# Expert weights as whole 2 MB units instead of pairs of 1 MB halves, with ring slots handed out whole

## The chip, the core and the metric

The kernel runs on one core of one Trainium2 chip. The metric is the device time of one execution in microseconds, given as the median of several runs. All data is 32-bit floating point.

## The reference, cut to what matters

The reference is a first network block of two layers (a gated-linear-attention and state-space mixer, then a dense feed-forward in layer 0 and a mixture of experts in layer 1), followed by a second block (Hyena convolution, neighbourhood attention, and a product-key expert lookup called PEER). The change lies in the mixture of experts:

```python
D_MODEL = 1024; SEQ = 256; D_FF = 3584; N_EXPERTS = 8; TOP_K = 2

def swiglu(t, w_gate, w_up, w_down):
    return (jax.nn.silu(t @ w_gate) * (t @ w_up)) @ w_down

def moe_swiglu(h, router_w, w_gate, w_up, w_down):
    t = h.reshape(bsz * seq, d)
    logits = (t @ router_w).astype(jnp.float32)
    top_v, top_i = lax.top_k(logits, TOP_K)
    top_p = jax.nn.softmax(top_v, axis=-1)
    gates = jnp.sum(jax.nn.one_hot(top_i, N_EXPERTS) * top_p[..., None], axis=1)
    out = jnp.zeros_like(t)
    for e in range(N_EXPERTS):
        out = out + gates[:, e:e + 1] * swiglu(t, w_gate[e], w_up[e], w_down[e])
    return out.reshape(bsz, seq, d)
```

Each of the 8 experts has three weight matrices of 1024 x 3584 values, so the stage reads 352 MB of weights once.

## The kernel before, in words

**Steps and units.** The hidden width 3584 of each expert is cut into 7 pieces of 512. An expert and a piece make a step, so the stage has 56 steps, n = 0 to 55. A step needs three units of weights of 2 MB each: `mg` (gate), `mu` (up) and `md` (down). In memory a unit fills 128 partitions with 16384 bytes each. Before the change every unit is stored, fetched, waited for and released as two halves (h = 0 and 1) of 1 MB, with 8192 bytes for each partition.

**Wide and small experts.** The tokens that chose an expert are gathered with matmuls, the expert works on the gathered tokens only, and the result is scattered back. Four experts are "wide" (up to 128 tokens) and four are "small" (up to 64 tokens). After the first expert, which is wide, the kernel ranks the others by load at run time and gives the fuller ones the wide places, so the row numbers of their weights are known only on the chip. That is why the units of steps 2 to 55 are fetched by an indirect DMA from GpSimd. The step list `TURNS[0].steps` has four blocks of 13 steps (one wide step, and then six times a wide and a small one) and four small steps at the end.

**Work of a step on TensorE.** In order: gate (`mg` of n), up (`mu` of n), down (`md` of n - 1), and a transposition of the activations. For a wide step each weight half is first split into a rounded high part, by a copy on ScalarE (`expert_high`, L2650, issued through the helper at L2483), and a low part, by a subtraction on VectorE (`expert_low`, L2042). Then TensorE makes three matmuls in place of one (`three`, L798 to L800). For a small step TensorE reads the fetched half directly (L1186 for gate and up, L1220 for down). Where an expert ended two steps earlier, `combine` (L1236 for wide, L1243 for small experts) multiplies its result back to the tokens in two portions, and VectorE adds it to the residual (`xT`, L1752).

**The weight ring.** Five slots of 16384 bytes per partition hold the weights. The class `Ring` hands them out in turn. `place` gives a whole slot and `place_half` gives half a slot, so the experts' stage has ten half slots. Each half has a semaphore for its arrival, and the last matmul that reads it marks it as empty (`done`). A new fetch into a half slot waits for that mark (`ring.free`). The units come in the order mg(0), mu(0), mg(1), mu(1), md(0), mg(2), and so on. Each unit therefore takes the place of the unit five earlier, and each half that of the half ten earlier.

**Who issues what.** SyncE issues the units of steps 0 and 1. GpSimd issues the other 324 halves in a row (L2996 to L3003), each as one `indirect_dma_start` behind its wait:

```python
for unit in moe_units(0):
    w, _, n, h = unit
    x, f = TURNS[0].steps[n]
    if n > 1:
        for used in ring.free(unit):
            e.wait_ge(*used)
        e.indirect_dma_start(ring.buf[unit], None, T[moe_table[w]], bass.IndirectOffsetOnAxis(
            m.rows[:, RANK[x], 2 * f + h:2 * f + h + 1], 0)).then_inc(ring.loaded[unit][0], 16)
```

On ScalarE a step n does, in this order: copy the activations of step n - 1, split `mu` of n (second half), split `md` of n - 1, apply Silu, split `mg` of n + 1 and the first half of `mu` of n + 1. VectorE follows with the low parts in about the same order, and it does `combined` after the low parts of `md`. Both engines work strictly in their order. If the number of tokens exceeds what the wide and small places hold, a flag makes the kernel run a second turn over all experts. This turn does not run with these inputs, but it has loads of its own on SyncE.

Of the kernel before, what the change touches and what calls it, by code (L numbers as in the profile page):

```python
# [10 lines left out]
ALU = mybir.AluOpType  # L11
# [18 lines left out]
def layout(items):  # L30
    at, out = 0, {}
    for name, n in items:
# [13 lines left out]
CS, NCS = layout([("ident", 128), ("ones", 128), ("bones", 128), ("perm", 128), ("tri", 128), ("iota", 128),  # L46
                  ("iota16", 16), ("scan64", 256), ("scan128", 256), ("iota8", 8), ("unit_rows", 14)])
MS, NMS = layout([("gla", 128), ("ssd", 128), ("col", 256)])
# [76 lines left out]
class Ring:  # L125
# [32 lines left out]

    def place_fetched(self, name):

        self.place_half(name)
        h = self.half[name]
        self.bytes[h] -= 16
        self.fetched[h] += 16
        self.loaded[name] = (self.fetch_sems[h], self.fetched[h])

# [109 lines left out]
def program(nc, T):  # L277
    with ExitStack() as ctx:
# [47 lines left out]
        def cst(name, rows=128, cols=None):  # L326
            o, n = CS[name]
            return cs[0:rows, o:o + (cols or n)]
# [109 lines left out]
        def moe_memory():  # L438
# [28 lines left out]
            m.ranked, m.part = (buf(64).rearrange("p (r e) -> p r e", r=8) for _ in range(2))  # L467
            m.rows = buf(112).bitcast(I32).rearrange("p (r n) -> p r n", r=8)
            m.flag = small[:, 24:26]
# [102 lines left out]
        def moe_units(turn):  # L572

            for i in range(57):
                if i < 56:
                    for w in ("mg", "mu"):
                        for h in range(2):
                            yield w, turn, i, h
                if i:
                    for h in range(2):  # L580
                        yield "md", turn, i - 1, h
        def ffn_units():

            for f in range(8):
                if f < 7:
                    for h in range(2):
                        for w in ("gate", "up"):
                            yield w, f, h
                if f:
                    for h in range(2):  # L590
                        yield "down", f - 1, h
# [31 lines left out]
        def sp(e):  # L623
# [6 lines left out]
            def load_half(name, src):  # L630
                base, loaded = ring.place_half(name)
                for used in ring.free(name):
                    e.wait_ge(*used)
                e.dma_start(base, src).then_inc(loaded, 16)
# [41 lines left out]

            def experts(turn):
                for unit in moe_units(turn):
                    w, _, n, h = unit
                    x, f = TURNS[turn].steps[n]  # L680
                    src = T[moe_table[w]][1792 * x + 256 * f + 128 * h:1792 * x + 256 * f + 128 * h + 128, :]
                    if turn:
                        base, loaded = ring.place_again(unit)
                        for used in ring.free(unit):
                            e.wait_ge(*used)
                        e.dma_start(base, src).then_inc(loaded, 16)
                    elif n < 2:
                        load_half(unit, src)
                    else:
                        ring.place_fetched(unit)  # L690

            experts(0)
            kept = ring.n, dict(ring.held)
            e.wait_ge(*V["flag"])
            with e.If(e.value_load(mo.over, min_val=0, max_val=1)):
                e.wait_ge(*P["moe done"])
                e.wait_ge(*V["moe done"])
                e.wait_ge(*A["moe done"])
                experts(1)
                e.wait_ge(*V["x", "moe"])  # L700
# [1000 lines left out]
        def dve(e):  # L1701
            def v(inst, name=None):
                V.mark(inst, name)
                e.wait_ge(*V.now)
# [305 lines left out]
            def rank():  # L2010
# [9 lines left out]
                                  cst("iota8").unsqueeze(1).to_broadcast([128, 8, 8]), ALU.is_equal))  # L2020
                v(e.tensor_scalar(m.chosen_by, m.chosen_by, 1792.0, None, ALU.mult))
                v(e.tensor_tensor(m.rows, m.chosen_by.unsqueeze(2).to_broadcast([128, 8, 14]),
                                  cst("unit_rows").unsqueeze(1).to_broadcast([128, 8, 14]), ALU.add), "unit rows")
                for src, dst in ((m.pos, m.posr), (m.g8, m.gr)):
# [944 lines left out]
        def pool(e):  # L2969
# [25 lines left out]
            e.wait_ge(*V["unit rows"])  # L2995
            for unit in moe_units(0):  # L2996
                w, _, n, h = unit
                x, f = TURNS[0].steps[n]
                if n > 1:
                    for used in ring.free(unit):  # L3000
                        e.wait_ge(*used)
                    e.indirect_dma_start(ring.buf[unit], None, T[moe_table[w]], bass.IndirectOffsetOnAxis(  # L3002
                        m.rows[:, RANK[x], 2 * f + h:2 * f + h + 1], 0)).then_inc(ring.loaded[unit][0], 16)  # L3003
            m = se2
# [32 lines left out]
def constants():  # L3037
# [15 lines left out]
    put(cs, CS, "iota8", np.tile(np.arange(8, dtype=f), (128, 1)))  # L3053
    put(cs, CS, "unit_rows", (p[:, None] + 128 * np.arange(14)[None, :]).astype(f))
    t = np.arange(256)
# [138 lines left out]
```

## Time and profile before

| what | value |
|---|---|
| median of 3 runs | 2486.24 us (2485.21 to 2486.52) |
| profiled execution: span from first to last instruction | 2482.8 us |
| experts' fetches by GpSimd, first to last issue | 599.2 to 1418.8 us |
| TensorE busy over the span | 92% |
| GpSimd fetches in the experts' stage | 324 of 1 MB |

The page gives the profiled execution by its span. A run's time holds that span and some microseconds before the first and after the last instruction, here 3.4 us from the span to the median. Times inside the execution are counted from the start of the span. The busy shares of the page are means over stages that have different limits, so they need to be read by stretches.

### The profile page before, as it was taken

Reading aid. Unit: us, or ns where it says so; the run is one execution under the profiler, and the core shown is the slowest. Engines: PE = TensorE matmul, PEld = TensorE weight load, DVE = VectorE, ACT = ScalarE, POOL = GpSimd, SP = SyncE. Lnnn points to the kernel's source line nnn. Section 1 sums busy time; section 2 is a strip of 40 time slices with the busy share of each in tenths; the row PEclk is TensorE's granted clock in tenths of the full one; section 3 lists DMA queues with packets and bytes.
Section 4 is the critical chain, followed back from the end, with each engine's and each line's share of the span. In section 5 each row is a group of like instructions: output and inputs, shape, how many; then the busy total and the mean of one; then the engine's idle time right before and its main releaser. Section 6 shows DMA issues by size and latency. Waiting matters only on the chain.

```text
span 2482.8 us, 31197 instructions
## 1 busy us (share of the span) xinstructions
PE 2287.0 (92%) x11674; PEld 1614.6 (65%) x11674; DVE 1615.4 (65%) x2656; ACT 994.3 (40%) x1627; POOL 749.1 (30%) x602
## 2 busy tenths in 40 slices
PE   5999999999999999999999989998899998877777
PEld 4789999788777777767776567676774544322222
DVE  6868995776556665655755135457578877777764
ACT  2334443334445544444544131013435544444443
POOL 0000000001665665556665400000023443433331
PEclk9999999998999999999999989999899999999999
DMA  9655867464999999999999973045389999999997
GB/s 378 253 205 231 325 265 286 170 238 178 397 421 421 407 415 419 391 421 421 381 421 419 420 292 136 34 160 228 138 340 395 420 421 420 421 422 421 421 421 314
DMA packets 108846, 824.71 MB, mean 332 GB/s; under 512 B 11904, under 2 KB 14208, under 8 KB 15504
## 3 DMA queue, kind: packets, MB, share of 16 engines
q0 software_dynamic: 83520, 608.21, 59.4%
q1 hardware_dynamic: 24448, 212.19, 21.7%
q10 hardware_dynamic: 720, 2.25, 0.3%
q8 instruction: 94, 1.54, 0.2%
q14 instruction: 64, 0.52, 0.1%
HBM read 821.55 MB, written 1.05 MB: 331 GB/s over the span
## 4 chain that ended last, share of the span: by engine, by line
PE 68%; DMA 16%; DVE 10%; issue 3%; ACT 2%; POOL 0%; SPq 0%; DVEq 0%; ACTq 0%; POOLq 0%
PE ps L798 9%; PE ps L800 9%; PE ps L799 9%; DMA arena<-in_uv,arena 8%; PE ps L784 7%; PE ps L1186 7%; DMA ring<-in_uv,arena 7%; PE ps L862 6%; PE ps L817 4%; PE ps L1220 4%; PE ps L1693 3%; DVE accb L2459 2%; PE ps L792 2%; ACT arena L2483 1%; PE ps L1030 1%
## 5 line engine op out<-in xcount | busy, mean ns | idle before, releaser
L2042 DVE TENSOR_TENSOR ring_r<-ring,arena_r 128x2048 fp32r<-128x2048 f32 x168 | 385.1, 2292 | 58.2 <-ACT arena_r L2483 53.8
L2483 ACT ACTIVATE arena_r<-ring 128x2048 fp32r<-128x2048 f32 x210 | 402.6, 1917 | 33.6 <-DMA ring<-in_ffn_w_down 15.7
L2483 ACT ACTIVATE arena<-arena 128x1 f32<-128x1 f32 (+6 forms) x617 | 187.9, 305 | 416.8 <-DVE arena L2459 307.4
L1693 PE MATMUL ps<-ring,sel 128*128 128x512 f32 x568 | 273.0, 611 | 61.2 <-ACT sel L2483 60.8
L3018 POOL DMA_INDIRECT ring<-in_uv,arena x142 | 133.3, 938 | 581.8 <-DVE arena L2313 340.7
L2483 ACT ACTIVATE arena<-ps 128x256 f32<-128x256 f32 (+1 forms) x228 | 105.7, 464 | 432.5 <-PE ps L792 138.1
L1693 PE MATMUL ps<-arena,sel 128*128 128x512 f32 x456 | 219.3, 609 | 43.5 <-ACT sel L2483 43.1
L798 PE MATMUL ps<-arena_r 128*128 128x512 f32 (+1 forms) x672 | 242.8, 361 | 0.4 <-DVE ring_r L2042 0.3
L1693 PEld LDWEIGHTS ps<-ring,sel 128*128 128x128 f32 x568 | 100.1, 190 | 213.6 <-ACT sel L2483 130.8
L2459 DVE CUSTOM_DVE_ANT_0 accb<-ring,ps 128x1024 f32<-128x1024 f32 x142 | 173.4, 1221 | 84.3 <-DMA ring<-in_uv,arena 80.4
L3002 POOL DMA_INDIRECT ring<-in_moe_w_gate,arena x108 | 164.7, 1525 | 149.7 <-PE ps L800 99.0
L3002 POOL DMA_INDIRECT ring<-in_moe_w_down,arena x108 | 168.1, 1556 | 113.2 <-PE ps L1186 70.7
L799 PE MATMUL ps<-arena_r 128*128 128x256 f32 x672 | 192.1, 286 | 0.0
L1693 PEld LDWEIGHTS ps<-arena,sel 128*128 128x128 f32 x456 | 80.6, 190 | 168.3 <-ACT sel L2483 98.7
L3002 POOL DMA_INDIRECT ring<-in_moe_w_up,arena x108 | 158.3, 1466 | 96.1 <-PE ps L1220 47.6
L2459 DVE CUSTOM_DVE_ANT_0 accb<-arena,ps 128x1024 f32<-128x1024 f32 x114 | 139.2, 1221 | 64.4 <-DMA arena<-in_uv,arena 62.5
L800 PE MATMUL ps<-arena_r 128*128 128x512 f32 x448 | 175.1, 391 | 0.0
L799 PE MATMUL ps<-ring_r,arena_r 128*128 128x512 f32 x448 | 174.8, 390 | 0.0
L862 PE MATMUL ps<-h,ring 128*128 128x256 f32 (+1 forms) x608 | 143.9, 396 | 11.8 <-ACT h L2483 5.5
L3018 POOL DMA_INDIRECT arena<-in_uv,arena x114 | 107.3, 942 | 146.2 <-PE ps L1693 126.6
L798 PEld LDWEIGHTS ps<-arena_r 128*128 128x128 f32 x672 | 127.3, 189 | 26.7 <-issue 10.2
L862 PEld LDWEIGHTS ps<-h,ring 128*128 128x128 f32 (+1 forms) x608 | 116.8, 195 | 37.1 <-issue 19.1
(315 smaller groups left out, 4191.0 us busy)
## 6 DMA issues: line engine op xcount, KB each, us to landing
ring<-in_ada_w SPq DMA_DIRECT2D x24, 1024.0 KB, 9.5
ring<-in_ada_w SPq DMA_DIRECT2D x12, 2048.0 KB, 8.6
ring<-in_w_in SPq DMA_DIRECT2D x10, 2048.0 KB, 12.5
ring<-in_w_ada SPq DMA_DIRECT2D x8, 2048.0 KB, 7.9
ring<-in_ffn_w_gate SPq DMA_DIRECT2D x14, 1024.0 KB, 5.6
ring<-in_ffn_w_up SPq DMA_DIRECT2D x14, 1024.0 KB, 6.9
ring<-in_ffn_w_down SPq DMA_DIRECT2D x14, 1024.0 KB, 7.4
ring<-in_w_out SPq DMA_DIRECT2D x6, 2048.0 KB, 11.6
```

Of the source, the lines that this page charges most:

```text
L784: last = e.matmul(out, a, b, start=(i == 0), stop=(i == len(pairs) - 1))
L798: e.matmul(out, xs[0], ws[0], start=start, stop=False, skip_group_check=True)
L799: e.matmul(out, xs[0], ws[1], start=False, stop=False, skip_group_check=True)
L800: return e.matmul(out, xs[1], ws[0], start=False, stop=stop, skip_group_check=True)
L862: last = e.matmul(out, a, b, start=(i == 0), stop=(i == len(pairs) - 1))
L1186: last = e.matmul(b[64 * g:64 * g + 64, 0:256], xs[:, 4 * h + k, :], tile[:, k, 256 * g:256 * g + 256], start=(h == k == 0), stop=(h == 1 ...
L1693: last = e.matmul(ps.banks[2 * t + c], m.diag[:, i % NDIAG, :], rows[:, 1024 + 512 * c:1536 + 512 * c], start=(i % 128 == 0), stop=(i % 12 ...
L2042: v(e.tensor_tensor(ring_low[ring.half[unit]], ring.buf[unit], mo.high[unit_at[unit] % NHIGH].bitcast(F32), ALU.subtract), ("low", unit))
L2459: v(e.tensor_tensor_reduce(m.waste, row_buffer(i)[0][:, 0:1024], x, 1.0, 0.0, ALU.mult, ALU.add, m.dots[:, i:i + 1]), ("dots", i))
L2483: A.mark(e.activation(out, src, func, **kw), name)
L3002: e.indirect_dma_start(ring.buf[unit], None, T[moe_table[w]], bass.IndirectOffsetOnAxis(m.rows[:, RANK[x], 2 * f + h:2 * f + h + 1], 0)).t ...
L3018: e.indirect_dma_start(base, None, T["uv"], bass.IndirectOffsetOnAxis(m.index[t][:, n:n + 1], 0)).then_inc(row_sems[ROWS[i][0]], 16)
```

## The change

The units of the first turn become whole. A table row holds 4096 values instead of 2048, one fetch brings all 2 MB, and a new method `place_whole` gives it a slot of the ring. The fetch waits until both halves of the former content are empty. Both halves share one arrival semaphore, so whoever waits for either half waits for the whole unit. Splitting, matmuls and releases stay by halves. SyncE makes 6 loads of 2 MB in place of 12 of 1 MB for steps 0 and 1, and GpSimd makes 162 fetches in place of 324. The table of row numbers shrinks from 14 to 7 columns per expert, and the second turn reads its halves as slices out of the wider rows.

```diff
-    def place_fetched(self, name):
-        self.place_half(name)
-        h = self.half[name]
-        self.bytes[h] -= 16
-        self.fetched[h] += 16
-        self.loaded[name] = (self.fetch_sems[h], self.fetched[h])
+    def place_whole(self, unit, fetched):
+        s = self.order[self.n // 2 % len(self.order)]
+        self.n += 2
+        halves = (2 * s, 2 * s + 1)
+        self.buf[unit] = self.bufs[s]
+        self.before[unit] = list(dict.fromkeys(self.held[h] for h in halves if h in self.held))
+        sems, count = (self.fetch_sems, self.fetched) if fetched else (self.sems, self.bytes)
+        count[2 * s] += 16
+        self.loaded[unit] = (sems[2 * s], count[2 * s])
+        for i, h in enumerate(halves):
+            name = (*unit, i)
+            self.held[h] = name
+            self.buf[name], self.half[name], self.loaded[name] = self.halves[h], h, self.loaded[unit]
...
+        def whole_units():
+            for i in range(57):
+                if i < 56:
+                    for w in ("mg", "mu"):
+                        yield w, 0, i
+                if i:
+                    yield "md", 0, i - 1
...
+            for unit in whole_units():
+                ring.place_whole(unit, unit[2] > 1)
+                if unit[2] < 2:
+                    for used in ring.free(unit):
+                        e.wait_ge(*used)
+                    e.dma_start(ring.buf[unit], unit_rows(*unit)).then_inc(ring.loaded[unit][0], 16)
...
-                v(e.tensor_scalar(m.chosen_by, m.chosen_by, 1792.0, None, ALU.mult))
-                v(e.tensor_tensor(m.rows, m.chosen_by.unsqueeze(2).to_broadcast([128, 8, 14]),
-                                  cst("unit_rows").unsqueeze(1).to_broadcast([128, 8, 14]), ALU.add), "unit rows")
+                v(e.tensor_scalar(m.chosen_by, m.chosen_by, 896.0, None, ALU.mult))
+                v(e.tensor_tensor(m.rows, m.chosen_by.unsqueeze(2).to_broadcast([128, 8, 7]),
+                                  cst("unit_rows").unsqueeze(1).to_broadcast([128, 8, 7]), ALU.add), "unit rows")
...
-            for unit in moe_units(0):
-                w, _, n, h = unit
+            for unit in whole_units():
+                w, _, n = unit
                 x, f = TURNS[0].steps[n]
                 if n > 1:
                     for used in ring.free(unit):
                         e.wait_ge(*used)
                     e.indirect_dma_start(ring.buf[unit], None, T[moe_table[w]], bass.IndirectOffsetOnAxis(
-                        m.rows[:, RANK[x], 2 * f + h:2 * f + h + 1], 0)).then_inc(ring.loaded[unit][0], 16)
+                        m.rows[:, RANK[x], f:f + 1], 0)).then_inc(ring.loaded[unit][0], 16)
...
-    def halves(w):
-        return w.reshape(-1, 128, 2, 2048).transpose(0, 2, 1, 3).reshape(-1, 2048)
+    def unit_rows(w):
+        return w.reshape(-1, 4096)
```

## Rows read from the trace of the kernel before

**Rows 1.** The page: its span, and GB/s moved in 40 equal slices.
```profile
span 2482.8 us, 31197 instructions
...
GB/s 378 253 205 231 325 265 286 170 238 178 397 421 421 407 415 419 391 421 421 381 421 419 420 292 136 34 160 228 138 340 395 420 421 420 421 422 421 421 421 314
```

**Rows 2.** Windows: stretch, busy by engine (instructions), clock, DMA share, GB/s.
```profile
642.00:1421.00 779.00, 772.90 (x4418) 548.42 (x4417) 439.60 (x324) 356.62 (x277) 471.89 (x311) 1.00 1.00 413
1200.00:1230.00 30.00, 29.91 (x159) 21.74 (x159) 20.56 (x16) 13.15 (x9) 19.28 (x12) 1.00 0.90 350
1258.00:1286.00 28.00, 28.00 (x162) 19.56 (x160) 15.52 (x10) 13.44 (x11) 18.67 (x13) 1.00 1.01 420
```

**Rows 3.** Waits from 642 to 1421 us: total, times, longest.
```profile
PE ps L1243 <- DVE xT L1752: 5.4, 3, 2.4
...
ACT arena_r L2483 <- DMA ring<-in_moe_w_up,arena: 4.2, 7, 1.2
```

**Rows 4.** The chain that ended last, one pair of steps on TensorE.
```profile
656.13 7.06 PE ps L1186 x64
...
684.17 7.06 PE ps L1186 x64
```

**Rows 5.** Windows of stretches that move rows of 16384 bytes.
```profile
1465.00:1470.00 5.00, 5.00 (x24) 4.39 (x24) 0.00 (x0) 3.48 (x6) 1.48 (x2) 1.00 1.01 429
1530.00:1535.00 5.00, 5.00 (x22) 4.00 (x22) 4.60 (x9) 0.95 (x2) 0.00 (x0) 1.00 1.02 436
```

**Rows 6.** Timeline of GpSimd's fetches: start, duration, idle before and releaser.
```profile
1199.86 0.94 POOL L3002 DMA_INDIRECT ring<-in_moe_w_gate,arena  x1 [3.15 <-PE ps L800]
1202.58 0.93 POOL L3002 DMA_INDIRECT ring<-in_moe_w_gate,arena  x1 [1.78 <-PE ps L800]
```

**Rows 7.** Landing times of fetches, from the queries of L3002, whole stage.
```profile
DMA to landing us min/median/max: 7.7/10.3/19.0
```

**Rows 8.** Timeline from 713 us, `md` of wide step 7: ScalarE, VectorE, TensorE.
```profile
713.37 1.91 ACT L2483 ACTIVATE arena_r<-ring 128x2048 fp32r<-128x2048 f32 x1 [0.49 <-DMA ring<-in_moe_w_down,arena]
...
715.87 1.91 ACT L2483 ACTIVATE arena_r<-ring 128x2048 fp32r<-128x2048 f32 x1 [0.58 <-PE ps L1186]
...
717.88 2.29 DVE L2042 TENSOR_TENSOR ring_r<-ring,arena_r 128x2048 fp32r<-128x2048 f32 x1 [0.20 <-ACT arena_r L2483]
...
719.19 0.50 PE L798 MATMUL ps<-arena_r 128*128 128x512 f32 x1
```

**Rows 9.** Timeline from 1082 us, `md` of wide step 31, then `combine`.
```profile
1082.25 3.86 ACT L2483 ACTIVATE arena_r<-ring 128x2048 fp32r<-128x2048 f32 x2
...
1084.27 4.62 DVE L2042 TENSOR_TENSOR ring_r<-ring,arena_r 128x2048 fp32r<-128x2048 f32 x2 [1.25 <-ACT arena_r L2483]
...
1088.92 2.04 DVE L1752 SCALAR_TENSOR_TENSOR xT<-ps,mods,xT 128x256 f32<-128x256 f32 x4
...
1090.87 1.91 ACT L2483 ACTIVATE arena_r<-ring 128x2048 fp32r<-128x2048 f32 x1 [0.46 <-DMA ring<-in_moe_w_up,arena]
1091.11 0.49 PE L1243 MATMUL ps<-arena 64*128 64x256 f32 x2 [1.35 <-DVE xT L1752]
```

**Rows 10.** Timeline from 1313 us, `md` of wide step 46, then `combine`.
```profile
1313.86 1.91 ACT L2483 ACTIVATE arena_r<-ring 128x2048 fp32r<-128x2048 f32 x1 [0.57 <-DMA ring<-in_moe_w_down,arena]
...
1315.87 2.29 DVE L2042 TENSOR_TENSOR ring_r<-ring,arena_r 128x2048 fp32r<-128x2048 f32 x1 [0.19 <-ACT arena_r L2483]
...
1318.20 2.04 DVE L1752 SCALAR_TENSOR_TENSOR xT<-ps,mods,xT 128x256 f32<-128x256 f32 x4
...
1320.39 1.07 PE L1243 MATMUL ps<-arena 64*128 64x256 f32 x4 [2.41 <-DVE xT L1752]
```

**Rows 11.** Timeline of TensorE at the end of the stage.
```profile
1426.89 8.55 PE L1186 MATMUL ps<-ring,sel 128*64 128x256 f32 x64 [5.04 <-issue]
...
1439.77 3.65 PE L1220 MATMUL ps<-ring,arena 128*64 128x512 f32 x16 [0.52 <-ACT arena L2483]
```

**Rows 12.** Timeline of SyncE's queue behind the last unit.
```profile
1439.57 0.82 SPq L628 DMA_DIRECT2D ring<-in_w_in  x2
```

More of the change, by code:

```diff
@@ L46 @@
 CS, NCS = layout([("ident", 128), ("ones", 128), ("bones", 128), ("perm", 128), ("tri", 128), ("iota", 128),
-                  ("iota16", 16), ("scan64", 256), ("scan128", 256), ("iota8", 8), ("unit_rows", 14)])
+                  ("iota16", 16), ("scan64", 256), ("scan128", 256), ("iota8", 8), ("unit_rows", 7)])
 MS, NMS = layout([("gla", 128), ("ssd", 128), ("col", 256)])
@@ L467, in moe_memory @@
             m.ranked, m.part = (buf(64).rearrange("p (r e) -> p r e", r=8) for _ in range(2))
-            m.rows = buf(112).bitcast(I32).rearrange("p (r n) -> p r n", r=8)
+            m.rows = buf(56).bitcast(I32).rearrange("p (r n) -> p r n", r=8)
             m.flag = small[:, 24:26]
@@ L675, in sp, with unit_rows, experts_again @@
                                 load_half(("down", f - 1, h), T["ffn_w_down"][f - 1][:, 2048 * h:2048 * h + 2048])
-            def experts(turn):
-                for unit in moe_units(turn):
-                    w, _, n, h = unit
[L680 to L692, printed above, removed]
+            def unit_rows(w, turn, n):
+                x, f = TURNS[turn].steps[n]
+                return T[moe_table[w]][896 * x + 128 * f:896 * x + 128 * f + 128, :]
+            for unit in whole_units():
[4 more added lines that the diff above has]
+                    e.dma_start(ring.buf[unit], unit_rows(*unit)).then_inc(ring.loaded[unit][0], 16)
+            def experts_again():
+                for unit in moe_units(1):
+                    w, _, n, h = unit
+                    base, loaded = ring.place_again(unit)
+                    for used in ring.free(unit):
+                        e.wait_ge(*used)
+                    e.dma_start(base, unit_rows(w, 1, n)[:, 2048 * h:2048 * h + 2048]).then_inc(loaded, 16)
             kept = ring.n, dict(ring.held)
@@ L698, in sp @@
                 e.wait_ge(*A["moe done"])
-                experts(1)
+                experts_again()
                 e.wait_ge(*V["x", "moe"])
@@ L3053, in constants @@
     put(cs, CS, "iota8", np.tile(np.arange(8, dtype=f), (128, 1)))
-    put(cs, CS, "unit_rows", (p[:, None] + 128 * np.arange(14)[None, :]).astype(f))
+    put(cs, CS, "unit_rows", (p[:, None] + 128 * np.arange(7)[None, :]).astype(f))
     t = np.arange(256)
@@ L3163 @@
         "ffn_w_down": downs(x["ffn_w_down"][0]),
-        "moe_w_gate": halves(np.concatenate([cols(w) for w in x["moe_w_gate"][0]])),
-        "moe_w_up": halves(np.concatenate([cols(w) for w in x["moe_w_up"][0]])),
-        "moe_w_down": halves(downs(x["moe_w_down"][0].reshape(-1, 1024))),
+        "moe_w_gate": unit_rows(np.concatenate([cols(w) for w in x["moe_w_gate"][0]])),
+        "moe_w_up": unit_rows(np.concatenate([cols(w) for w in x["moe_w_up"][0]])),
+        "moe_w_down": unit_rows(downs(x["moe_w_down"][0].reshape(-1, 1024))),
         "w_ada": turned(x["w_ada_2"][0]), "w_in2": cols(x["w_in_2"][0]), "f4w": x["hy_f4_w_2"][0].reshape(64, 2, 2, 512).transpose(2, 0, 1, 3).reshape(128, 1024),
```

## The prediction

> **What bounds the kernel now.** I read the page's slices first. They show where transfers could matter: in 14 slices of about 62 us the core moves 391 to 421 GB/s, and that is the experts' stage [rows 1]. The stage looks bound by DMA. The windows contradict this, since from 642 to 1421 us TensorE is busy for 772.9 of 779.0 us, so it idles for 6.1 us in all, while DMA moves 413 GB/s on average [rows 2]. The list of waits says what that idle time is: 5.4 us are three waits of `combine` for VectorE, and ScalarE's longest kind of wait for a fetch adds up to 4.2 us in 7 times, none longer than 1.2 us [rows 3]. So TensorE sets the pace and DMA follows closely behind it. Both statements have to be held together, because a change in how weights arrive can take away at most those few microseconds, yet it can add stalls wherever the weights arrive just in time.
>
> How close is it? One wide and one small step take TensorE 28.04 us [rows 4]. They need six units of 2.097 MB, which at the 420 GB/s of a full stretch take 29.96 us [rows 2]. Within a block DMA therefore loses 1.9 us for each pair. At the seams between blocks, where two wide steps follow each other and experts are combined, TensorE takes longer. The ring fills, DMA pauses (350 GB/s from 1200 to 1230 us) and the lead is made up [rows 2]. The tight places are thus late in each run of pairs. I looked in the timelines for units whose split starts at the moment of landing, and found three places where TensorE is near: `md` of steps 7, 31 and 46 [rows 8 to 10].
>
> **The change part by part.** *Fewer and longer fetches.* GpSimd issues 162 in place of 324. One takes it 0.93 us or more [rows 6], and it is busy 471.9 of 779 us [rows 2]. This is off the path, because its wait for TensorE's releases covers it. I count 0. Behind a waiting fetch only later fetches are queued, and those need later releases anyway.
>
> *Rows of 16384 bytes.* For this queue the trace has no such row. The lower bound of the effect is nothing. For the upper side, SyncE's loads with these rows ran at 429 GB/s in one stretch and 436 in another [rows 5], against 420 for the half-length rows [rows 2]. I take 429, the longer-lasting state, which is 2% less time: a unit takes 4.89 us instead of 4.99. While DMA works without a pause it gains 2% of the time passed since the last refill.
>
> Here the row speaks for a gain and a rule speaks against it. The Trainium skill, page "DMA: Bandwidth & Descriptors", section "Specifications", gives 512 bytes as the smallest transfer for full rate. By that rule 8192 bytes are already far beyond it, the longer row brings nothing, and the sum is that of the second case below. The trace's 429 against 420 disagrees a little.
>
> *Whole arrival.* A half takes 2.5 us (1.049 MB at 420). So far ScalarE could copy the first half while the second was coming. Now both copies wait for the second. Only places without slack pay:
> - Step 7. The second half's copy starts on landing at 715.87. If the first copy started then, its subtraction would run from 717.88 and end at 720.17, while the first matmul started at 719.19 [rows 8]. That is 1.0 us late.
> - Step 31. The copies start at 1082.25 as a pair. The landing is read back from the next one that was waited for: 1090.87 is the third half after it, so 1090.87 - 3 x 2.5 = 1083.3 [rows 9]. The copies, the subtractions (4.62 us), the four additions and `combine` all move by 1.05 us, which lengthens its wait of 1.35.
> - Step 46. The second half lands at 1313.86. Today one subtraction follows and then the additions. With both halves landing together there are two, so additions and `combine` come 2.3 us later, and its wait of 2.41 grows by that [rows 10].
>
> *Whole release.* A slot is asked for only when its second half is empty. With releases 2.72 us apart in wide steps [rows 6] and 7.06/4 = 1.77 us in small ones [rows 4], the first unit of a refill starts 1.8 to 2.7 us later. Once DMA is behind, however, it always has other units queued (landings take 7.7 to 19.0 us after issue, while a half moves in 2.5 [rows 7]), and a late start there is invisible. What remains is a later start of each unbroken stretch. The bounds are 0 and 1.8 us (the small steps end the refill). I take 0.7, nearer to nothing, since today's second half of the same unit also comes only then.
>
> *The sum.* At step 7 DMA has been full for some 70 us and has gained 1.4: 1.0 + 0.7 - 1.4 = 0.3 us. At step 31 it has for some 53 us: 1.05 + 0.7 - 1.1 = 0.65. At step 46 for some 84 us: 2.3 + 0.7 - 1.7 = 1.3. Together that is 2.3 us more.
>
> *The rest.* SyncE's 12 loads become 6. The slots before them held whole tiles, so each pair of halves was issued together already. The mixer's matmuls and the routing cover the first one, and without that cover it would be 2.5 us once. The row table loses 56 columns of one VectorE instruction, and by 2.29 us for 2048 columns [rows 8] that is 0.06 us. At the end the last unit lands near 1439.5, when SyncE's next loads are let go [rows 12], and TensorE begins it at 1439.77, released by ScalarE [rows 11]. After 209 us at 2% less 0.7, it lands 3.5 us earlier. That helps nothing, because TensorE comes to it in its own order, behind a pause of 5.04 us for "issue" and 64 matmuls. Needing both halves at 1439.77 costs nothing either, if the unit is not later than now.
>
> The profiled execution has a span of 2482.8 us, so 2485.1 afterwards. The median is 3.4 us above that span, and 2486.2 + 2.3 = 2488.5 us.
>
> **The rivals.**
> - *The longer row moves no faster* (or the queue cuts it into two of 8192 bytes, so that the change doesn't do all that it says). No gain accrues: 1.7 + 1.75 + 3.0 us at the three places and 0.5 at the end, 7.0 in all, 2493.2 us. Slower. Speaking for it is that no row of GpSimd's queue has this length; against it are the 429 and 436 [rows 5]. It decides as soon as the unit's time is not below 4.95 us.
> - *The ring is too coarse.* Five slots behave like four and a half, and each restart is a full 1.8 us late, without a faster row: 2.8 + 2.85 + 4.1 at the three places and 1.6 at the end, 11.4 us, 2497.6 us. For it: ten places against five. Against it: landings 10.3 us after issue in the middle show a deep queue [rows 7].
> - *Row at 436 GB/s.* That is 3.7% less time: 2.6, 2.0 and 3.1 us gained. The first place is safe, the others end at -0.25 and -0.1. If DMA comes early by more, the wait of 2.41 us vanishes, and no more than that, since the other waits of `combine` are not for a landing: 2485.9 down to 2483.8 us. No change that can be told.
> - *DMA is the bound after all.* Then 162 units save 0.10 us each, 16 us, 2470 us. For it: a DMA share of 1.00 over 779 us. Against it: TensorE's 6.1 us of idle time, which cannot give 16.
>
> **How the numbers follow.** Chances: forecast 0.52, no faster row 0.18, too coarse 0.08, 436 GB/s 0.15, DMA-bound 0.07. A measurement can tell about 0.2%, 5.0 us, from no change, so the limits are 2481.3 and 2491.2. The forecast and the 436 case are inside but for 0.02, and of the no-faster-row case 0.05 falls inside: same 0.70. Slower is 0.13 + 0.08 + 0.02 = 0.23, faster 0.07. The range goes from 2483.8, all of the removable wait, to 2494.0, just above the slower case. It leaves out the coarse ring, the DMA bound and some 0.04 more, which is about 0.19.
>
> **What the profile after would show.** A GB/s row of 428 to 430 in full stretches of the stage (420: second case). 162 fetches. TensorE's idle time from 642 to 1421 us at some 8 us in place of 6.1, with the waits of `combine` (L1243) grown from 5.4 to about 7.4 us and a new short wait of L798 for L2042 near 719 us. ScalarE's waits for the fetches should rise above their present sum, harmlessly. The last unit's landing should come some microseconds before TensorE asks for it. The prediction is wrong if the copies' delays run on into Silu or the copy of activations, which stand behind them on ScalarE and which I have counted as covered, or if GpSimd's long fetches open gaps between units.

## The result, and the profile after

| kernel | median | runs | ratio to before, 95% interval |
|---|---|---|---|
| before | 2486.38 us | 2485.21 to 2491.18 | |
| changed | 2509.99 us | 2506.23 to 2515.24 | 1.009 (1.0078 to 1.0103) |

The change makes the kernel slower by 0.9%. The prediction said 2488.5 us, at most 2494.0, and most likely no change that can be told. It was wrong. The profiled execution of the changed kernel took 2511.57 us and has a span of 2509.8 us, 27.0 more than before.

The page and the windows of the changed kernel, which answer to [rows 1, 2] and add three stretches (columns as there):

```profile
span 2509.8 us, 31192 instructions
...
GB/s 374 249 204 237 328 267 265 179 224 184 414 418 402 399 387 415 383 386 419 376 427 388 428 331 134 36 105 240 176 309 382 421 421 421 421 422 421 421 421 310
```

```profile
642.00:1421.00 779.00, 756.16 (x4245) 541.29 (x4243) 438.69 (x318) 357.20 (x275) 189.11 (x150) 0.98 0.97 403
1258.00:1286.00 28.00, 27.98 (x159) 19.54 (x158) 14.07 (x10) 11.99 (x11) 8.57 (x7) 1.00 1.01 428
...
866.00:894.00 28.00, 24.39 (x102) 17.47 (x102) 15.54 (x15) 8.28 (x6) 5.78 (x4) 0.88 0.82 327
1090.00:1118.00 28.00, 23.51 (x137) 15.76 (x134) 17.03 (x16) 13.43 (x10) 7.13 (x5) 0.88 0.87 367
1342.00:1370.00 28.00, 28.00 (x144) 19.65 (x142) 13.66 (x12) 8.15 (x7) 5.58 (x4) 0.93 0.83 340
```

Three things stand in these rows. A full stretch now moves 428 GB/s in place of 420, which is the 2% that was forecast. The queue doesn't cut the longer rows in two either: from 1258 to 1286 us it moves 11.96 MB in 816 packets, where before moved 11.76 MB in 1614.
The waits of the changed kernel from 600 to 1460 us (total, times, longest) say what TensorE waits for:

```profile
ACT arena_r L2501 <- DMA ring<-in_moe_w_down,arena: 39.8, 17, 3.8
...
ACT arena_r L2501 <- DMA ring<-in_moe_w_up,arena: 28.2, 22, 3.2
ACT arena_r L2501 <- DMA ring<-in_moe_w_gate,arena: 20.3, 22, 2.6
...
PE ps L1261 <- ACT arena_r L2501: 12.7, 3, 4.5
...
PE ps L816 <- DVE ring_r L2060: 10.0, 10, 1.9
```

L1261, L816 and L2501 are L1243, L798 and L2483 of before. The three waits of `combine` grew from 5.4 to 12.7 us [rows 3]. Of the ten waits at L816 eight, with 9.4 us, are new: they stand at the first matmul of a wide `md`. Two of 0.31 us each are there in before too. ScalarE's copies wait 88.3 us in 61 times for a landing, the longest 3.8 us, where the longest kind of before had 4.2 us in 7 [rows 3]. At each of these copies the unit has no lead: it is asked for before it has landed.

One of the three places, in the timelines of ScalarE, VectorE and TensorE (start, duration, work, idle before and releaser), `md` of step 16 and then `combine`:

```profile
860.76 3.85 ACT L2501 ACTIVATE arena_r<-ring 128x2048 fp32r<-128x2048 f32 x2 [2.11 <-DMA ring<-in_moe_w_down,arena]
...
862.77 4.62 DVE L2060 TENSOR_TENSOR ring_r<-ring,arena_r 128x2048 fp32r<-128x2048 f32 x2 [3.33 <-ACT arena_r L2501]
867.42 2.04 DVE L1770 SCALAR_TENSOR_TENSOR xT<-ps,mods,xT 128x256 f32<-128x256 f32 x4
...
861.16 1.13 PE L1261 MATMUL ps<-arena 64*128 64x256 f32 x8
862.23 3.67 PE L1204 MATMUL ps<-ring,sel 128*64 128x256 f32 x32
869.61 2.08 PE L1261 MATMUL ps<-arena 64*128 64x256 f32 x8 [3.71 <-ACT arena_r L2501]
871.62 0.79 PE L816 MATMUL ps<-arena_r 128*128 128x512 f32 x1
872.21 0.63 PE L817 MATMUL ps<-ring_r,arena_r 128*128 128x512 f32 x1
872.64 0.63 PE L818 MATMUL ps<-arena_r 128*128 128x512 f32 x1
```

It is read from left to right in time. The fetch lands at 860.7, two copies and two subtractions follow, then the additions of the first portion (867.42), and only after them do the banks come free for the second portion of `combine`, which TensorE could have begun at 865.9. It waits 3.71 us. The row names a copy of ScalarE as the releaser, because that copy ends last by the profile (865.65 and 3.85 is 869.50), but the additions end at 869.46, almost together with it. That the additions are what counts is shown further down, where moving them takes the wait away. The wait is not all. Eight matmuls of L1261 took 1.13 us before the wait and 2.08 after it, and the 128 x 512 matmuls start 0.43 us apart (872.21 and 872.64), where they start 0.23 us apart elsewhere. The clock has fallen to the lower of its two levels: from 870 to 874 us the granted clock is 0.50. In before the same two copies ran at 853.83, right behind the work ahead of them and with no wait for a landing:

```profile
853.83 3.85 ACT L2483 ACTIVATE arena_r<-ring 128x2048 fp32r<-128x2048 f32 x2
```

GpSimd's fetches at the start of the stage, first of before, then of the changed kernel, show where that lead (the time between the landing of a unit and its first use) goes:

```profile
606.01 0.94 POOL L3002 DMA_INDIRECT ring<-in_moe_w_up,arena  x1 [1.46 <-PE ps L800]
619.56 2.43 POOL L3002 DMA_INDIRECT ring<-in_moe_w_gate,arena  x1 [12.62 <-PE ps L800]
...
636.36 2.48 POOL L3002 DMA_INDIRECT ring<-in_moe_w_gate,arena  x1 [0.31 <-issue]
```

```profile
607.92 0.94 POOL L3020 DMA_INDIRECT ring<-in_moe_w_up,arena  x1 [4.19 <-PE ps L818]
624.17 0.94 POOL L3020 DMA_INDIRECT ring<-in_moe_w_gate,arena  x1 [15.30 <-PE ps L818]
629.61 0.94 POOL L3020 DMA_INDIRECT ring<-in_moe_w_up,arena  x1 [4.50 <-PE ps L810]
633.88 1.23 POOL L3020 DMA_INDIRECT ring<-in_moe_w_down,arena  x1 [3.33 <-PE ps L1204]
```

The restart at 619.56 moved to 624.17. Of these 4.6 us, 1.4 come from ahead of the stage's steps (TensorE's first transpositions there begin at 606.66 in before and now at 608.06), so 3.2 us are the change's. In the changed kernel each of the next fetches stands behind a release of TensorE too. In before some wait for "issue" only (636.36), which means that their place was empty already. From 600 to 642 us DMA moved 290 GB/s in place of 330.

### The profile page after: what moved, and what is told of

It is laid out like the page before. It is cut to its first block, busy times and chain, and to the rows that moved or that the text cites. A ratio compares the mean times of both kernels' runs of the same rounds, so it can differ in the third digit from the quotient of the medians.

```text
span 2509.8 us, 31192 instructions
## 1 busy us (share of the span) xinstructions
PE 2294.8 (91%) x11674; PEld 1619.7 (65%) x11674; DVE 1615.9 (64%) x2656; ACT 994.7 (40%) x1627; POOL 461.9 (18%) x440
## 3 DMA queue, kind: packets, MB, share of 16 engines
HBM read 821.54 MB, written 1.05 MB: 328 GB/s over the span
## 4 chain that ended last, share of the span: by engine, by line
PE 63%; DMA 21%; DVE 9%; issue 4%; ACT 3%; POOL 0%; SPq 0%; DVEq 0%; ACTq 0%; POOLq 0%
DMA ring<-in_uv,arena 13%; PE ps L816 9%; PE ps L818 9%; PE ps L817 9%; PE ps L802 7%; PE ps L880 6%; PE ps L1204 5%; DMA ring<-in_moe_w_down,arena 4%; PE ps L835 4%; PE ps L1711 4%; PE ps L1238 2%; DMA arena<-in_uv,arena 2%; DVE accb L2477 1%; DMA ring<-in_moe_w_gate,arena 1%; ACT arena_r L2501 1%
## 5 line engine op out<-in xcount | busy, mean ns | idle before, releaser
L2501 ACT ACTIVATE arena_r<-ring 128x2048 fp32r<-128x2048 f32 x210 | 402.6, 1917 | 112.4 <-DMA ring<-in_moe_w_down,arena 39.8
L2501 ACT ACTIVATE arena<-arena 128x1 f32<-128x1 f32 (+6 forms) x617 | 188.0, 305 | 424.6 <-DVE arena L2477 306.9
L2501 ACT ACTIVATE arena<-ps 128x256 f32<-128x256 f32 (+1 forms) x228 | 105.9, 465 | 380.4 <-PE ps L810 108.8
L816 PE MATMUL ps<-arena_r 128*128 128x512 f32 (+1 forms) x672 | 244.5, 364 | 9.8 <-DVE ring_r L2060 9.7
L816 PEld LDWEIGHTS ps<-arena_r 128*128 128x128 f32 x672 | 128.5, 191 | 37.6 <-DVE ring_r L2060 13.2
L1782 DVE CUSTOM_DVE_ANT_0 arena<-ring,accb,pv 128x1024 f32<-128x1024 f32 x96 | 123.4, 1285 | 20.5 <-DMA ring<-in_ada_w 13.4
L816 PE MATMUL ps<-h_r,arena_r 128*128 128x256 f32 x448 | 130.2, 291 | 5.5 <-DVE ring_r L1766 3.4
L817 PEld LDWEIGHTS ps<-arena_r 128*128 128x128 f32 x672 | 131.3, 195 | 0.0
## 6 DMA issues: line engine op xcount, KB each, us to landing
ring<-in_w_in SPq DMA_DIRECT2D x10, 2048.0 KB, 12.7
```

The costliest lines, as they stand in the source:

```text
L816: e.matmul(out, xs[0], ws[0], start=start, stop=False, skip_group_check=True)
L817: e.matmul(out, xs[0], ws[1], start=False, stop=False, skip_group_check=True)
L1782: v(e.tensor_tensor_reduce(t.waste, tile[:, m, :], s, 1.0, pvc(t.bias, o), ALU.mult, ALU.add, out[:, o:o + 1]))
L2501: A.mark(e.activation(out, src, func, **kw), name)
```

## The experiments

All are ratios to runs of the kernel before on the same chips. "us" is the ratio less 1, times 2486. The medians of before in these groups are 2486.38 us (changed kernel), 2488.23 (e1 to e4), 2488.46 (e5, e6, e7 and e9) and 2487.74 (e10, e11), so the ratios, and not the bare medians, are to be compared. An interval spans 2 to 4.5 us to either side, so a difference of two kernels of under some 3 us is not clear of noise.

| kernel | median | ratio, 95% interval | us |
|---|---|---|---|
| e1, whole release alone | 2501.17 | 1.0042 (1.0028 to 1.0056) | +10.4 |
| e2, whole arrival alone | 2497.36 | 1.0028 (1.0019 to 1.0037) | +7.0 |
| e3, both | 2515.92 | 1.0110 (1.0092 to 1.0128) | +27 |
| changed kernel (both, and long rows) | 2509.99 | 1.0090 (1.0078 to 1.0103) | +22 |
| e5, before with additions split | 2486.73 | 0.9997 (0.9988 to 1.0006) | -0.7 |
| e6, e1 with additions split | 2491.79 | 1.0017 (1.0009 to 1.0026) | +4.2 |
| e7, e2 with additions split | 2490.49 | 1.0009 (1.0000 to 1.0017) | +2.2 |
| e11, e3 with additions split | 2501.53 | 1.0052 (1.0038 to 1.0066) | +12.9 |
| e4, changed kernel with additions split | 2494.34 | 1.0027 (1.0015 to 1.0038) | +6.7 |
| e9, e4 with halves in wide steps | 2490.75 | 1.0007 (0.9998 to 1.0015) | +1.7 |
| e10, before with a slower combine | 2499.12 | 1.0045 (1.0031 to 1.0059) | +11.2 |

My first theory after the result was that the lead of the ring is lost through whole slots, and that the stalls at `combine` are made dearer by the clock. The rivals were the arrival by itself, the long rows or fetches by themselves, and a stage bound by DMA.

### The parts of the change one by one (e1, e2, e3)

e1 lets the two fetches of a unit wait together, in the kernel before (SyncE's loads of steps 0 and 1 too):

```diff
                 if n > 1:
-                    for used in ring.free(unit):
-                        e.wait_ge(*used)
+                    for u in ((w, 0, n, 0), (w, 0, n, 1)) if h == 0 else ():
+                        for used in ring.free(u):
+                            e.wait_ge(*used)
```

> Kernel before, with one part of the change: the two 1 MB fetches of a unit both wait until both halves of the slot are empty. Arrival, rows of 8192 bytes and everything else stay as before. Lost lead (my theory): the release is what costs, because a fetch starts only after the second half of its place is read, so the ring refills later in the wide and small pairs and TensorE meets a unit just landing. About 2498 us (2493 to 2505), with new waits of L798 on VectorE and more waiting of L2483 on DMA. Arrival alone (rival): this run stays at 2486 to 2489. Long rows or long fetches (rival): this run stays at 2486 to 2488 as well, since rows and fetches are those of before.

e2 lets each reader of a first half (L1182, L1215 and L2647) wait for the second too:

```diff
+                        if h == 0:
+                            arrived((w, turn, n, 1))
                         arrived((w, turn, n, h))
...
+                if h == 0:
+                    e.wait_ge(*ring.loaded[w, turn, i, 1])
                 e.wait_ge(*ring.loaded[unit])
```

> Kernel before, with another part alone: whoever needs the first half of a unit also waits for its second half. The fetches stay 1 MB each and are released by halves. Lost lead: nothing of the lead is lost, since a half is used about 10 us after it landed, except where the trace of before showed margins under 3 us; 2488 to 2491 us. Arrival alone (rival): the copies to the high part start up to 2.5 us later and the delays add, 2500 to 2510 us. Long rows or long fetches (rival): 2486 to 2488.

e3 has both edits.

> Kernel before with both parts: a slot is released whole and a unit arrives whole, but it is still two fetches of 1 MB with rows of 8192 bytes. It differs from the changed kernel by the row length alone. Lost lead: a unit comes each 4.99 us in place of 4.89, and in most of a block TensorE runs at the pace of the DMA, so this is slower than the changed kernel: 2516 us (2511 to 2526). Long rows or long fetches as the cause (rival): close to before, 2486 to 2492.

Rows of the waits from 600 to 1460 us, first of e1, then e2, then e3:

```profile
ACT arena_r L2491 <- DMA ring<-in_moe_w_down,arena: 23.4, 21, 3.7
...
PE ps L1251 <- DVE xT L1760: 10.9, 3, 5.1
...
PE ps L806 <- DVE ring_r L2050: 2.9, 5, 1.8
```

```profile
ACT arena_r L2487 <- DMA ring<-in_moe_w_down,arena: 14.2, 9, 3.6
...
PE ps L1247 <- ACT arena_r L2487: 8.1, 2, 5.0
PE ps L798 <- DVE ring_r L2046: 2.2, 4, 1.3
PE ps L1247 <- DVE xT L1756: 1.4, 1, 1.4
```

```profile
ACT arena_r L2495 <- DMA ring<-in_moe_w_down,arena: 38.2, 15, 4.3
...
PE ps L1255 <- ACT arena_r L2495: 13.7, 3, 5.6
PE ps L806 <- DVE ring_r L2054: 11.6, 9, 2.1
```

e3 lands on its expectation, 2516: the waits and the slow-down are there with rows of 8192 bytes and 1 MB fetches, so neither row length nor fetch size is the cause. The changed kernel differs from e3 by one fetch of 2 MB with long rows in place of two of 1 MB, and this is a gain of 5 us (27.3 less 22.4), though the two intervals overlap. Row length and fetch size were not varied apart, and where this text speaks of the worth of longer rows it means both. e1 is inside its expected range. e2 is not: 2497.36 is 6 us above the 2491 of my theory's range, and near the rival's 2500. Arrival counts too. But the rival's reason, delays in every wide step, doesn't hold either, since TensorE waits only 2.2 us in four places for low parts, and 9.5 us at `combine` (8.1 and 1.4). So two parts that cost 10.4 and 7.0 us cost 27.3 together, 10 more than their sum, and in all three the largest wait is the one at `combine`. That asked for a kernel without that wait.

### The combine's wait taken away (e4)

In the changed kernel, the additions of the first two pairs go ahead of the low parts of `md`:

```diff
+                    if n in plan.combined:
+                        combined(plan.combined[n], (0,))
                     if plan.wide_at(n - 1):
                         low("md", n - 1, 0)
                         low("md", n - 1, 1)
                     if n in plan.combined:
-                        combined(plan.combined[n])
+                        combined(plan.combined[n], (1,))
```

> The changed kernel with one edit on VectorE: in the step that combines an expert, the residual adds of the first two pairs stand ahead of the low parts of md, those of the last two behind them as before. The second portion of the combine (L1261) then has its banks before md's low parts are made. Lost lead with a clock that falls after the stalls: the three stalls of 3.7, 4.5 and 4.5 us shrink to under 1.5 each, the granted clock behind them stays at 0.98 or more where it was 0.88 to 0.95, and some 4 us come back as waits for late md units, since the stall had let the ring refill: 2497 us (2492 to 2502). Clock that falls for another reason (rival): about 2502 with the clock rows unchanged. All bound by the DMA (rival): 2507 to 2510, since every removed stall comes back as a wait for a unit.

The same place in e4, first TensorE, then the window over it and the waits:

```profile
866.18 1.14 PE L1261 MATMUL ps<-arena 64*128 64x256 f32 x8
867.26 0.48 PE L816 MATMUL ps<-arena_r 128*128 128x512 f32 x1
```

```profile
866.00:894.00 28.00, 26.77 (x146) 18.73 (x144) 17.82 (x14) 12.63 (x9) 5.33 (x5) 1.00 0.99 408
```

```profile
PE ps L816 <- DVE ring_r L2060: 13.0, 14, 1.7
```

2494.34 us, 15.7 under the changed kernel and inside the expected 2492 to 2502. The second portion now starts at 866.18 without a wait and takes 1.14 us, the clock stays at 1.00, and in the same 28 us TensorE is busy for 26.77 us at the full clock in place of 24.39 us at 0.88. Three stalls of 12.7 us together left. Of that, 3.0 us came back at L816 behind VectorE (10.0 to 13.0), 1.2 at L816 behind ScalarE and 0.8 in a wait for a fetch, so 7.7 us of stall are worth 15.7 us. Most of the rest belongs to the clock: the changed kernel has four falls of it up to 1410 us and e4 has none. This first one costs about 2.4 us: 0.94 in L1261 (2.08 less 1.14), and 1.5 in the next nine matmuls, whose starts reach over 3.68 us (871.62 to 875.30) in place of 2.17 (867.26 to 869.43). The DMA-bound rival is out for this kernel, as it allowed at most 3 us.

### The same without the combine's wait (e5, e6, e7, e11)

> The kernel before with the edit of e4 on VectorE (residual adds of the first two pairs ahead of the low parts of md). The three waits at L1243 of before (1.63, 1.35 and 2.41 us between two matmuls) go, and the clock of 0.94 after the third one stays at 1.00; up to 1.2 us each come back as a wait of the first L798 of md on its low part, as in e4. About 3 to 5 us under before. Rival (the DMA sets the pace, so that a removed stall comes back): within 1 us of before.

> e1 (whole release alone) with the edit of e4. If the combine, together with the clock behind it, is where the lost lead becomes time, this lands near 2491 us (2488 to 2495), 10 us under e1. If the release costs by itself in every pair of steps (rival), it stays at 2496 to 2500.

> e2 (whole arrival alone) with the edit of e4. Combine and clock as the place where the delay becomes time: near 2487 us (2484 to 2490), 10 us under e2. Rival, arrival costs by the copies' delays in every wide step: 2493 to 2496.

> e3 (whole release and whole arrival, two fetches of 8192-byte rows) with the edit of e4. Against e4, which has the longer rows, it gives their worth a second time. By e3 and the changed kernel the longer rows are worth 6 us: 2500 us (2496 to 2504), 15 under e3. If they are worth the whole 2% on all fetches behind step 2, it would be 2508; if they are worth nothing without the combine's stall, 2494.

e6, e7 and e11 are where the theory put them or within 1 us of its range (2491.79, 2490.49, 2501.53), and outside the rivals' 2496 to 2500 and 2493 to 2496. Without the combine's wait, release costs 4.2 us, arrival 2.2 and both 12.9. They still cost more than their sum, now by 6.5 us (some 4 to 5 us of uncertainty by the intervals), so the `combine` is not the only place where the two meet. Waits of e6, e7 and e11 from 600 to 1460 us show another, the low parts:

```profile
PE ps L806 <- DVE ring_r L2050: 7.3, 8, 1.6
```

```profile
PE ps L798 <- DVE ring_r L2046: 7.7, 7, 2.0
```

```profile
PE ps L806 <- DVE ring_r L2054: 15.5, 12, 3.0
```

With the additions split and nothing else changed (e5) this wait is 4.4 us. Release adds 2.9 us to it, arrival 3.3 and both 11.1, which is 4.9 more than their sum. Behind the wait of 2.99 us in e11 (725.46) the clock fell as well, for an estimated 1.3 us (7 matmul starts over 3.03 us in place of 1.69). The longer rows are worth 6 us again (12.9 less 6.7), and again the intervals touch. Two pairs that agree make the gain likely, and its size stays rough.

e5 went the other way than I expected. The 5.4 us of waits in before go, and nothing is gained: 2486.73, 0.9997. Its waits, in the stretch from 600 to 1460 us:

```profile
PE ps L1186 <- issue: 5.1, 1, 5.1
...
PE ps L798 <- DVE ring_r L2042: 4.4, 5, 1.3
```

Most of the wait moved to L798 (0.6 us in before, 4.4 now). The trace tells how much was taken back where, if both kernels are laid over each other at TensorE's transpositions, which close each step (counted from 606.66 us in before and 609.99 in e5). The three `combine` steps of a small expert run 1.6, 1.4 and 4.1 us faster, and in the step behind each of them 1.5 us are lost again. The first of these losses, on ScalarE, VectorE and TensorE, and one at the end of the stage:

```profile
861.51 5.81 ACT L2485 ACTIVATE arena_r<-ring 128x2048 fp32r<-128x2048 f32 x3
870.21 6.94 DVE L2042 TENSOR_TENSOR ring_r<-ring,arena_r 128x2048 fp32r<-128x2048 f32 x3
872.65 0.47 PE L798 MATMUL ps<-arena_r 128*128 128x512 f32 x1 [1.27 <-DVE ring_r L2042]
...
1417.28 1.95 PE L1186 MATMUL ps<-ring,sel 128*64 128x256 f32 x16 [0.31 <-DMA ring<-in_moe_w_up,arena]
```

ScalarE's copies are done at 867.3, so no landing is involved. VectorE is late by its own queue of additions and low parts, and this same wait of 1.2 to 1.3 us stands behind the three `combine` steps of every kernel with the split. At the transposition at 1411.21 e5 is still 2.7 us ahead. Then TensorE waits for an `up` and two `down` fetches (0.31, 0.62 and 0.46 us), and the next transposition comes after 12.91 us, where it comes after 10.86 in before. That leaves 0.6 us. So the rival was right in its number, but of the gain VectorE's order takes back 4.5 us and the pace of the fetches 2.1 (one profiled execution of each). The pause of 5.1 us before the last small step stayed as well [rows 11], and no row says what it waits for.

### Halves where a lead is needed (e9)

A second table of row numbers lets the wide steps' units go by halves again, while the small steps' stay whole:

```diff
+                    for name, src, at in ((unit, table, m.rows[:, RANK[x], f:f + 1]),) if whole(unit) else [
+                            ((*unit, h), table.rearrange("r (h c) -> (r h) c", h=2),
+                             m.rows2[:, RANK[x], 2 * f + h:2 * f + h + 1]) for h in range(2)]:
+                        for used in ring.free(name):
+                            e.wait_ge(*used)
```

> The changed kernel with the edit of e4, but units of wide steps go by halves of 8192 bytes for a partition again (fetch, release and arrival), and only the units of the small steps stay whole 2 MB. A second table of row numbers serves the halves. Lost lead: whole units cost nothing where TensorE reads them directly some 5 to 10 us after landing, and the wide ones have their lead back: 2484 us (2481 to 2488), with 0 to 3 us of waits of L816 on VectorE where the changed kernel has 10. Rival, any whole unit takes the depth from the ring for all that follow: 2489 to 2494.

2490.75 us is in the rival's range and above my theory's. By the ratios 5.0 of the 7.4 us between e4 and e5 came back. The last 2.4 would be the cost of whole units in the small steps alone, but the intervals of e9 and e5 overlap. The waits for low parts (L837 here) were 13.0 us in 14 in e4 and are 5.7 in 7, not 0 to 3. In e5 they are 4.4, so most of what is left of them is VectorE's order.

```profile
PE ps L837 <- DVE ring_r L2084: 5.7, 7, 1.3
...
PE ps L1225 <- DMA ring<-in_moe_w_up,arena: 1.2, 1, 1.2
```

The second row points at the place. Where the small steps follow each other at the end of the stage, TensorE reads the whole units directly and waits for three of them itself: `gate` 0.66 us, `up` 1.23 and `down` 1.23, between 1410 and 1421 us. From transposition to transposition this step takes 14.48 us, where it took 12.91 in e5 and 10.86 in before. The theory had put these units 5 to 10 us ahead of their use. Here they are late.

### A longer combine in the kernel before (e10)

The last question was whether a stall at `combine` costs more than itself, with ring and fetches as before:

```diff
                     if n in plan.combined:
+                        if plan.wide_at(n - 1):
+                            v(e.tensor_tensor(xT, xT, xT, ALU.max))
                         combined(plan.combined[n])
```

> The kernel before, with its ring and fetches untouched, and one more instruction on VectorE in the three steps that combine a small expert (a maximum of xT with itself, 2048 columns, about 2.3 us, ahead of the residual adds). The waits at L1243, 1.63, 1.35 and 2.41 us in before, grow to about 3.9, 3.6 and 4.7. If a wait of this length there costs itself and a lower clock after it (my reading of the changed kernel), the clock behind the three falls to 0.88 to 0.94 for about 28 us each and the time is 3 to 10 us above before: 7 of stalls and 4 to 7 of clock, less up to 5 that the wait for the last small experts' weights gives back. Rival (the stage is paced by its fetches, a stall at the combine is made up for): within 2 us of before, and the clock rows too stay.

Waits from 600 to 1460 us, TensorE behind the third place, and two windows:

```profile
PE ps L1243 <- DVE xT L1752: 12.3, 3, 4.7
```

```profile
1331.28 2.08 PE L1243 MATMUL ps<-arena 64*128 64x256 f32 x8 [4.69 <-DVE xT L1752]
1333.28 0.79 PE L798 MATMUL ps<-arena_r 128*128 128x512 f32 x1
```

```profile
866.00:894.00 28.00, 28.00 (x142) 19.61 (x142) 14.70 (x12) 7.21 (x6) 10.88 (x10) 0.93 0.85 336
...
1314.00:1342.00 28.00, 23.31 (x131) 14.83 (x131) 18.52 (x17) 11.69 (x10) 13.88 (x9) 0.88 0.95 396
```

The three waits grew by 6.9 us to 12.3, nearly the 12.7 of the changed kernel, and the time by 11.2 us, which is 1 us above the 3 to 10 that I had expected: the pause before the last small step gave back 0.8 us and not up to 5. The clock fell behind each of the three waits, where it fell behind one in before. So a microsecond added at this wait costs about 1.6 us. This rules out that the stage makes up for a stall there, and gives the `combine` with its clock about half of the changed kernel's 22 us by itself.

## Why the prediction was wrong, point by point

- **What bounds the kernel.** Right as far as it went: TensorE sets the pace, DMA follows closely, and the tight places are late in each run of pairs. (The full slices of [rows 1] are 13 with 381 to 421 GB/s, not 14 with 391 to 421, which changes nothing.) At the very end of the stage DMA has no slack even in before: as soon as TensorE came 2.7 us earlier there (e5), it waited for fetches. The working even has the number that should have warned: DMA loses 1.9 us for each pair. The lead of the ring is what pays for that, and I never worked out how much of it there is.
- **Fewer and longer fetches, 0 us.** Not tested alone; GpSimd's busy time fell from 471.9 [rows 2] to 189.1 us, and no unit waits for its issue.
- **Rows of 16384 bytes at 429 GB/s.** Right: 428. The worth of the long rows, together with the single 2 MB fetch, is 5 to 6 us (e3 and e11 against the changed kernel and e4), where the sum had 4.2. The rule of the Trainium skill (page "DMA: Bandwidth & Descriptors", section "Specifications") that 512 bytes are enough for full rate would make it 0. Here 8192-byte rows move 420 GB/s and 16384-byte rows 428 in the same queue, and the measurement decides.
- **Whole arrival, 1.0, 1.05 and 2.3 us.** The sizes hold as stalls: in e2 the three waits at `combine` are 9.5 us in place of 5.4, 4.1 more where 3.35 was forecast, and near 720 us there is one short wait at L798. But they cost 7.0 us, not 4.35. The granted clock in the windows from 1090 to 1118 and from 1314 to 1342 us of e2 is 0.94 and 0.88, where before has 1.00 and 0.94.
- **Whole release, 0.7 us for each stretch.** This is the step that failed: "a late start there is invisible. What remains is a later start of each unbroken stretch." I took 0.7 us for it. The first restart was 3.2 us later, each of the fetches from 624.17 to 633.88 waits for TensorE, and at the `md` split of the first `combine` step the copies ran 6.9 us later than before (860.76 against 853.83). TensorE itself was 4.9 us later by then (857.56 against 852.71), so the copies lost 2.1 us against it, which is their wait of 2.11 us for the landing. The row that I had leant on could not have shown this. The landing in the middle went from 10.3 [rows 7] to 12.4 us after issue, and less the transfer itself (2.5 and 4.9) that is 7.8 and 7.5, almost the same. The bound of 1.8 us was too low as well, and with it the "ring is too coarse" rival (2497.6 us, 0.08), which named the right mechanism. What release costs alone is 10.4 us (e1).
- **The sum as a sum.** Release and arrival were added at three places. They lengthen the same waits and draw on the same lead, and together cost 27 us where each by itself costs 10 and 7.
- **The clock.** It is not in the working at all. Row and rule were both at hand: the window from 1314 us in before has the clock at 0.94 behind the wait of 2.41 us. The Trainium skill, page "TensorE: Matmul & The Clock Gate", section "What's actually happening", says that an idle stretch sends the array back from 2.4 to 1.2 GHz. The traces agree for most long waits, with starts of 128 x 512 matmuls 0.43 us apart after the wait and 0.23 otherwise, and the exceptions are listed at the end.

Of the 24.8 us by which the last `combine` of the stage starts later (1444.17 to 1468.94), 1.4 came from ahead of step 1, 7.3 are the longer waits at `combine`, 9.4 those at L816 (10.0 less 0.6), and the pause before the last small step is 0.5 shorter (4.5 in place of 5.0). That leaves 7.2 us. Four falls of the clock (behind the waits of 3.71, 4.49 and 4.50 us, and one behind a wait of 1.90 us at 1402.6) less the one that before has, at 2.4 us each, are an estimate of 7.2. (They are not equally dear: behind the wait of 1.90 us the `md` takes 7.19 us up to its transpositions, where it takes 5.55 at 724.08, so that fall cost 1.6.) The remaining 2.2 us of the span lie behind the stage, where the kernels are alike.

What stays open: how long each restart of DMA is late in the later blocks, as landings there were read only through who waits for them, and why release and arrival together lengthen the waits for low parts by more than their sum. That the lead of the ring is what both take away is read from who waits for a landing. No kernel with a deeper ring, which would test it, was tried, since the memory is taken.

No version here beats before. e5, which keeps the halves, can't be told from before, and among the kernels with whole units e9, which has them in the small steps alone, comes nearest.

## What to carry to other kernels

A ring's depth counts in places that are released one by one. Before making transfers larger at the same memory, work out the lead (places times the time of one) against the deficit that has to be carried between two refills; when the lead is just enough, coarser places cost more than a faster row gives, here 27 us against 5.

Costs that draw on the same slack don't add. Price them together at the place where slack ends, and count a TensorE wait of several microseconds with the slower clock behind it, here 1.6 us for each added microsecond.

A wait that looks removable may only be where the slack shows: taking away 5.4 us in before gained nothing, because the next engine and the fetches were as late, and taking away 12.7 in the changed kernel gained 15.7.

## What the runs showed of the hardware

- The granted clock fell behind most waits of TensorE of 2.3 to 5.6 us in this stage, and once 1.5 us after the end of a wait of 1.90 us (the matmuls starting at 1403.64 and 1404.22 in the changed kernel took 0.39 and 0.63 us). It did not after waits of 1.63 and 1.35 us in before, nor after one of 2.12 us (clock 1.00 from 1258 to 1342 us) and one of 3.21 us at 870.65 in e3, where the next eight matmuls took 1.14 us and the clock is 1.00 from 866 to 894 us. So the length of a wait alone did not decide it. One fall cost 1.6 to 2.4 us.
- In GpSimd's queue rows of 16384 bytes moved 428 GB/s and rows of 8192 bytes 420, with fetches of 2 MB and 1 MB. e3 and e11 against their partners give a gain in time of 5 and 6 us, each at the edge of the noise.
- A fetch of 2 MB landed 8.7 us after its issue at the least (4.9 us of it are the transfer at 428 GB/s), a fetch of 1 MB 7.7 us in before and 5.4 in e3 (2.5 us of transfer). So even in the quickest fetch of a kernel an estimated 3 to 5 us pass besides the transfer.
